# Entering a run of 256-column matmuls: six half-width products against one idle 352-column product, and a bank alignment moved

## The reference

```python
x = x + mix @ w_out[l]
h = rms_norm(x, norm_mlp[l])
x = x + jnp.square(jax.nn.relu(h @ w_up[l])) @ w_down[l]
```

## Time and profile before

| | |
|---|---|
| median of three runs | 1761.58 us |
| profiled execution, its time | 1762.81 us |
| its span, first to last instruction | 1761.0 us |
| TensorE matmul busy | 1751.4 us (99%) |
| TensorE weight loads | 1536.5 us (87%) |
| VectorE busy | 1233.6 us (70%) |
| ScalarE busy | 846.5 us (48%) |
| GpSimd busy | 38.2 us |
| DMA | 176.61 MB, mean 100 GB/s |

### The profile page before, as it was taken

The page is one execution under the profiler, slowest core; times in us unless marked ns, Lnnn a source line. Parts: engine busy times, 40 slices in busy tenths (PEclk is TensorE's granted clock), DMA queues, the critical chain, the costliest instruction groups (busy, mean ns, idle before and its releaser), DMA issues.

```text
span 1761.0 us, 26584 instructions
## 1 busy us (share of the span) xinstructions
PE 1751.4 (99%) x10407; PEld 1536.5 (87%) x10407; DVE 1233.6 (70%) x1949; ACT 846.5 (48%) x1436; POOL 38.2 (2%) x38
## 2 busy tenths in 40 slices
PE   9999999999999999999999999999999999999998
PEld 7889989878888899988888998988877788989897
DVE  7849849666776557965794894975677676848474
ACT  6425626454333335743453562654655443627274
POOL 0000000000000000000000000000222000000000
PEclk9999999999999999999999999999999999999999
DMA  5233423432123232333323233334421233333232
GB/s 185 73 116 97 131 86 103 121 98 84 59 77 104 90 102 97 109 120 96 96 84 120 84 114 103 106 106 133 135 69 49 84 96 96 97 96 119 91 115 72
DMA packets 68427, 176.61 MB, mean 100 GB/s; under 512 B 8112, under 2 KB 9392, under 8 KB 68304
## 3 DMA queue, kind: packets, MB, share of 16 engines
q1 hardware_dynamic: 66576, 171.60, 31.3%
q10 hardware_dynamic: 1280, 2.08, 0.3%
q0 software_dynamic: 448, 1.24, 0.3%
HBM read 170.70 MB, written 2.10 MB: 98 GB/s over the span
## 4 chain that ended last, share of the span: by engine, by line
PE 97%; DVE 1%; ACT 1%; issue 0%; DMA 0%; DVEq 0%; ACTq 0%; POOLq 0%
PE ps L2045 19%; PE ps L2047 19%; PE ps L2046 19%; PE ps L2131 10%; PE ps L2133 10%; PE ps L2132 10%; PE ps L2067 2%; PE ps L2069 2%; PE ps L2068 2%; PE ps L2410 0%; PE ps L2421 0%; PE ps L2435 0%; PE ps L2280 0%; PE ps L2077 0%; PE ps L2283 0%
## 5 line engine op out<-in xcount | busy, mean ns | idle before, releaser
L2045 PE MATMUL ps<-Ahi,wh 128*128 128x512 f32 x913 | 358.9, 393 | 0.9 <-DVE Alo L1836 0.6
L2046 PE MATMUL ps<-Alo,wh 128*128 128x512 f32 x913 | 355.4, 389 | 0.0
L2047 PE MATMUL ps<-Ahi,wl 128*128 128x512 f32 x913 | 355.4, 389 | 0.0
L2131 PE MATMUL ps<-BThi,wh 128*128 128x256 f32 x1232 | 341.7, 277 | 0.9 <-ACT tm L569 0.7
L2132 PE MATMUL ps<-BTlo,wh 128*128 128x256 f32 x1232 | 340.7, 277 | 0.0
L2133 PE MATMUL ps<-BThi,wl 128*128 128x256 f32 x1232 | 340.6, 276 | 0.0
L543 ACT ACTIVATE wh<-raw 128x1024 fp32r<-128x1024 f32 (+1 forms) x206 | 213.2, 1036 | 228.6 <-PE ps L2047 195.2
L1147 DVE TENSOR_TENSOR wl<-raw,wh 128x1024 fp32r<-128x1024 f32 (+1 forms) x206 | 248.6, 1208 | 66.1 <-ACT wh L543 63.9
L2131 PEld LDWEIGHTS ps<-BThi,wh 128*128 128x128 f32 x1232 | 231.6, 188 | 2.7 <-DVE wl L1154 2.0
L2133 PEld LDWEIGHTS ps<-BThi,wl 128*128 128x128 f32 x1232 | 231.4, 188 | 0.0
L2132 PEld LDWEIGHTS ps<-BTlo,wh 128*128 128x128 f32 x1232 | 231.3, 188 | 0.0
(11 more groups left out here) (345 smaller groups left out, 2701.5 us busy)
## 6 DMA issues: line engine op xcount, KB each, us to landing
raw<-in_w_gu SPq DMA_DIRECT2D x128, 256.0 KB, 2.8
raw<-in_w_d SPq DMA_DIRECT2D x32, 512.0 KB, 3.6
raw<-in_w_dn SPq DMA_DIRECT2D x32, 512.0 KB, 3.9
raw<-in_w_up SPq DMA_DIRECT2D x48, 256.0 KB, 2.8
raw<-in_w_gu SPq DMA_DIRECT2D x22, 512.0 KB, 3.6
raw<-in_w_d SPq DMA_DIRECT2D x16, 384.0 KB, 3.1
raw<-in_w_v SPq DMA_DIRECT2D x8, 512.0 KB, 4.0
raw<-in_w_cc SPq DMA_DIRECT2D x8, 512.0 KB, 3.6
```

The source lines that it names most:

```text
L2045: pe.matmul(ps, wh[:, c], hi[:, k, :], start=(k == 0), stop=False)
L2046: pe.matmul(ps, wh[:, c], lo[:, k, :], start=False, stop=False)
L2047: last = pe.matmul(ps, wl[:, c], hi[:, k, :], start=False, stop=(k == nb - 1))
L2131: pe.matmul(ps, whi[:, w], bhi, start=(new and kp == 0), stop=False, skip_group_check=not new)
```

## The change

Three things are changed. The halves are gone: every unit does all its blocks with 512 columns. In the same nine places the pair now begins with one more matmul: 352 columns of `BThi` (product c = 0, slices 0 and 1 taken as one row of 512 and cut at 352) with the weights of the first real matmul, into the bank that this first matmul then overwrites; its result is used by nobody. For the first pair of a layer it waits for two slices of `bl`, where the first real matmul waits for one. And the alignment of the bank counter in the SwiGLU layers is moved from the first pair of the third group (`at % 7 == 5`) to the first down unit of the third group (`at % 7 == 2`).

```diff
         if u in PAIR:
             PREVP[u], last = last, u
-            if name in ("w_gu1", "w_gu2") and n == FG[2][0]:
-                while at % 7 != 5:
-                    at += 1
             bs = [bank(7) for _ in range(3)]
...
         EV0.append(done)
+        if name in ("w_d1", "w_d2") and n == 0 and k1 == FT:
+            while at % 7 != 2:
+                at += 1
         if banks == 0:
...
-            halves = u + 1 in PAIR and layer(u) != 1
...
-                if halves and k == nb - 1:
-                    for t in (LEFT, RIGHT):
-                        pe.matmul(ps[:, t], wh[:, c], hi[:, k, t], start=False, stop=False)
-                        pe.matmul(ps[:, t], wh[:, c], lo[:, k, t], start=False, stop=False)
-                        last = pe.matmul(ps[:, t], wl[:, c], hi[:, k, t], start=False, stop=(t == RIGHT))
-                    continue
                 pe.matmul(ps, wh[:, c], hi[:, k, :], start=(k == 0), stop=False)
...
                     if first and c == 0:
                         pe.wait_ge(s["bl"], 4 * layer(p) + kp + 1)
+                    if c == 0 and kp == 0 and p - 2 not in PAIR and layer(p) != 1:
+                        if first:
+                            pe.wait_ge(s["bl"], 4 * layer(p) + 2)
+                        pe.matmul(BK[BANK[p][b]][:, 0:352], whi[:, w],
+                                  BThi[:, c, 0:2, :].rearrange("p k t -> p (k t)")[:, 0:352], start=True, stop=True)
                     pe.matmul(ps, whi[:, w], bhi, start=(new and kp == 0), stop=False, skip_group_check=not new)
```

## The result

The changed kernel takes 1776.69 us (median of four, 1776.56 to 1778.67) against 1761.69 us (four runs) of the kernel before: a ratio of 1.0087, 95% interval 1.0068 to 1.0104. The forecast was 1764.4 us, with 1767.0 as the end of the range. The time is that of rival B, 1777 us. The changed kernel's profiled execution took 1776.63 us with a span of 1774.8 us, 13.8 us more than the span before.

The account below looks back on a forecast made before the run. The prediction took the kernel to be bound by one stream of TensorE matmuls. Bank waits 2.06, idle matmuls 0.81 and hidden places -0.07 gave +2.8 us on 1761.58, so 1764.4 us, with a range of 1762.3 to 1767.0.

Parts of the forecast that it names:

- rival B: Pair runs entered from 512 columns by way of 352 stay at the slow pace: +15 us, 1777 us; chance 0.14.
- The halves as a cost of nothing: Before the nine pair runs: six 256-column matmuls become three of 512, counted as 0.04 us less a place.
- A: The main case: bank waits and idle matmuls cost +2.8 us in all, 1764.4 us; chance 0.74.
- No slow stretch began without a wait: In the trace before the change, slow stretches of pairs always begin behind a wait; given as the argument against slow entry.
- the prediction's own signs of being wrong: Long runs at 117 to 118 ns a matmul, a wait not on L1306, or MLP runs changed over 0.5 us each.
- The idle matmul: At nine pair-run entries: 0.156 us each, 0.116 net of the halves; seven places pay in full, 0.81 us.
- the two first runs hide it: First runs of both SwiGLU layers: a later wait covers the idle matmul, 2 x -0.03 = -0.07 us.
- The bank alignment: Down unit 0 of both SwiGLU third groups waits for L1306 to read the last pair's bank: 2 x 1.03 = 2.06 us.
- The paces behind waits: Each wait in a pair run draws fast or slow pace anew: -1.2 to +1.2 us on top of the sum.
- The skill's rule: Isolated gap of N/2.4 + 2.5 ns for N columns, so one pace only; by it the sum would be +3.0 us.
- the case that the rule excluded: Pair runs entered from 512 columns by way of 352 run at the slow pace: +15 us, 1777 us; chance 0.14.

Follow-up runs that it names:

- direct: The kernel before without the six 256-column halves in front of each pair run and with no idle matmul: 1774.11 against 1762.21 us, 1.0066.
- bank_only: The kernel before with only the bank alignment moved as in the change: 1763.78 against 1762.21 us, 1.0008.
- act_plus_64: The kernel before with Hhi, Hlo, Ahi and Alo moved by 64 bytes, weights and BThi left in place: 1792.77 us, 1.017.
- M_plus_64: The kernel before, halves kept, with the region that holds BThi, BTlo, MThi and MTlo moved by 64 bytes: 1787.48 us, 1.014.
- two_halves: The kernel before with only the last 512-column matmul before each pair run cut into two of 256: 1762.06 against 1762.79 us, 0.9996.

## Why the prediction was wrong, step by step

- **The halves as a cost of nothing.** This step failed. The prediction priced them by their columns, 0.04 us a place, and put their absence down as a gain. direct shows that leaving them out costs 12 us, since they decide the pace of up to 672 matmuls behind them.
- **The choice of A over B.** "No slow stretch began without a wait" was true of the trace, but every entry in that trace went through 256-column matmuls at the 120 ns pace first. That the direct step wasn't in the trace was written down, and should have made B as likely as A; it got 0.14. B's price was right: 10.4 us for the four long runs (measured 10.4), 2.0 for the MLP runs (measured 1.3, since a wait in the third pair ends the slow pace in all three), 15 in all. Of the prediction's own signs of being wrong, the first one came: long runs at 117.8 ns a matmul.
- **The idle matmul.** Forecast 0.156 us, measured 0.161. Right. Net of the halves a place costs 0.13 us, forecast 0.116. Seven places pay it and the two first runs hide it: measured -0.15 and -0.78 us in those runs, before their own entries of 0.13. The second of these is mostly the pace behind the waits.
- **The bank alignment.** Place, releaser and size were right: 0.85 us late and 0.09 of restart at both places of the changed kernel, 0.90 and about 0.1 in bank_only. (The bank's last user before the change is the fourth pair and not the fifth, which changes nothing.) This was the term that the sum rested on, and it is a seventh of the loss.
- **The paces behind waits.** The estimate of up to 1.2 us either way held: bank_only pays 2.0 us for its waits and shows 0.9 in its span. The reading behind it, that a slow stretch lasts, was too simple: in the kernel before, one of 24 matmuls begins at 911.6 us and turns fast at 914.5, behind a stall of a few ns (distances of 121 and 122) at the next product. And by the prediction's own bounds the idle matmul and the restart reach down to -0.6 us and not -0.4; the range holds either way.
- **The skill's rule.** The Trainium skill, "TensorE: Matmul & The Clock Gate" (Back-to-back issue gap), gives one isolated gap for a width. Here, in a stream, 256 columns cost 113.4, 116.7, 117.8, 118.3 or 120.0 ns at one clock, and 512 columns 226.7 or 233.3. So one gap for a width doesn't describe this stream, and the case that the rule excluded is the one that came.

What stays open is the mechanism. What is shown is that the pace depends on the operand's offset and on the widths issued before, and that with the same widths it can still differ, along with the distances in front (act_plus_64). That weight load and moving operand disturb each other at some relative phase would fit, but no run shows it.

## What to carry to other kernels

When a stream of matmuls is the bound, read its pace, not its durations, run by run: width of a window divided by the count. Work that looks idle at the border between two widths may be what sets the pace of everything behind it, so price its removal by all the matmuls of the run, and treat an entry that the trace doesn't hold as unknown. Entries are cheap to map: give each place of one kernel its own width and read them all from one trace.

## What the runs showed of the hardware

- A steady stream of 256-column matmuls whose operand lies 64 bytes off the weights' offset (modulo 128) has two paces, 113.4 and 117.8 ns, and keeps the one it entered with until a wait or another operand region (672 matmuls in a row).
- At the weights' own offset a steady stream of 256 columns costs 120.0 ns (in M_plus_64 everywhere) and one of 512 columns 226.7; only the first 256-column matmul behind 512 columns comes at 113 (two_halves). At 64 bytes off, 512 columns cost 233.3 on Ahi and Hhi (act_plus_64) and 229 on average on MGhi and MGlo (M_plus_64).
- One idle matmul of 352 columns leads to the slow pace, one of 448 to the fast one: 12 us of 1765 by one number.
- Behind a wait the second distance tells what follows: over all traces here with BThi at its old offset, 195 ns was followed by the fast pace in 40 of 41 cases and 192 ns by the slow one in 22 of 30; 193 and 194 by either.
